# Hybrid trunk step: one weight stream over five expert buffers, the overflow chunk as a fixed unit, the last pair's rows added on TensorE, and another key and query stage

## The reference

```python
def token_mixing(h, p, lru_h0, ctx_ckv, ctx_kr):
    z = h @ p['w_in']                       # Fourier, RG-LRU, short convolution, latent attention
    ...
    q = rmsnorm(einsum(rmsnorm(q_c, g_qa), w_qb), g_qn)   # 8 heads of 64 + 32 channels
    ckv = rmsnorm(kv_c, g_kva)
    k, v = mla_kv(ckv, k_r, w_kvb, g_kn)    # rms over 64 per-head + 32 shared rotary channels
    q, k = rope_tail(q), rope_tail(k)       # latent tokens only: the 32 tail channels are rotated
    ...                                     # 128 cached context keys are appended
    out = sum(gates * branches) @ w_out

def hier_moe(h, p):                         # 4 groups of 8 experts, top 1 group, top 2 experts
    a, u = t @ w1[e], t @ w3[e]             # 1024 -> 256, for each of 32 experts
    y = (silu(a) * u * combine) @ w2[e]     # 256 -> 1024
```

## Time and profile before

| | |
|---|---|
| median of three runs | 1210.94 us (1210.21 to 1211.07) |
| profiled execution, its own time | 1212.13 us |
| its span, first to last instruction | 1210.1 us |
| mean granted TensorE clock | 0.929 |
| TensorE matmul busy | 1019.2 us (84%) |
| VectorE, ScalarE, GpSimd busy | 352.9, 207.0, 190.5 us |
| DMA | 201.34 MB, mean 166 GB/s over the span |

### The profile page before, as it was taken

The page is one execution under the profiler, slowest core; times in us unless marked ns, Lnnn a source line. Parts: engine busy times, 40 slices in busy tenths (PEclk is TensorE's granted clock), DMA queues, the critical chain, the costliest instruction groups (busy, mean ns, idle before and its releaser), DMA issues.

```text
span 1210.1 us, 10632 instructions
## 1 busy us (share of the span) xinstructions
PE 1019.2 (84%) x4116; PEld 582.2 (48%) x4116; DVE 352.9 (29%) x689; ACT 207.0 (17%) x376; POOL 190.5 (16%) x185
## 2 busy tenths in 40 slices
PE   3899989977699899999999999899456987887770
PEld 1455545634355467777777777445432332332320
DVE  4214331235445413233223332134410111111116
ACT  3104430022155410111011111011001111111110
POOL 0000100024520111213131221011010110111102
PEclk9999999989799999999999999899568998899995
DMA  9552551020000252122212121701545899999936
GB/s 374 236 197 93 196 199 44 1 81 0 1 1 1 88 221 84 44 87 69 71 45 95 44 96 60 305 35 60 201 134 209 317 425 425 426 424 427 421 159 260
DMA packets 34657, 201.34 MB, mean 166 GB/s; under 512 B 7408, under 2 KB 11184, under 8 KB 22960
## 3 DMA queue, kind: packets, MB, share of 16 engines
q1 hardware_dynamic: 29840, 190.17, 39.8%
q0 software_dynamic: 4768, 10.49, 2.5%
HBM read 193.37 MB, written 14.09 MB: 171 GB/s over the span
## 4 chain that ended last, share of the span: by engine, by line
PE 80%; DVE 7%; issue 5%; DMA 4%; ACT 2%; POOL 2%; SPq 0%; ACTq 0%; DVEq 0%; POOLq 0%
PE psum L878 20%; PE psum L999 11%; PE psum L623 8%; PE psum L895 7%; PE psum L929 6%; PE psum L1015 5%; PE psum L739 3%; PE psum L815 2%; DMA r_w<-in_w_ada 2%; PE psum L624 2%; PE psum L632 2%; PE psum L829 2%; PE psum L839 2%; PE psum L726 1%; PE psum L773 1%
## 5 line engine op out<-in xcount | busy, mean ns | idle before, releaser
L878 PE MATMUL psum<-r_h,r_w 128*128 128x320 f32 x512 | 143.3, 433 | 1.7 <-DVE r_d L1594 1.7
L1927 POOL TENSOR_TENSOR r_w<-r_w 128x512 f32<-128x512 f32 x64 | 80.6, 1270 | 315.5 <-PE psum L878 240.4
L878 PEld LDWEIGHTS psum<-r_h,r_w 128*128 128x128 f32 x512 | 97.2, 190 | 42.4 <-DVE r_d L1594 2.0
L878 PE MATMUL psum<-r_ys,r_w 128*128 128x320 f32 x384 | 108.6, 432 | 0.0
L623 PE MATMUL psum<-r_h,r_w 128*128 128x512 f32 x192 | 100.2, 604 | 1.5 <-DVE r_h L1376 1.5
L878 PEld LDWEIGHTS psum<-r_ys,r_w 128*128 128x128 f32 x384 | 73.0, 190 | 30.4
L999 PE MATMUL psum<-r_a,r_ckv 128*64 128x512 f32 x128 | 68.2, 694 | 19.8 <-issue 18.6
L1237 ACT ACTIVATE r_bv<-r_bv 128x320 f32<-128x320 f32 x64 | 30.1, 470 | 272.8 <-DVE r_bv L1641 272.8
L929 PE MATMUL psum<-r_w,r_bv 128*128 128x512 f32 x160 | 72.1, 612 | 3.4 <-DVE r_bv L1636 3.4
L999 PE MATMUL psum<-r_w,lruw 128*64 128x512 f32 x128 | 59.1, 616 | 17.0 <-issue 17.0
L999 PE MATMUL psum<-r_c,r_ckv 128*64 128x512 f32 x128 | 68.3, 695 | 0.0
(11 more groups left out here) (342 smaller groups left out, 1499.6 us busy)
## 6 DMA issues: line engine op xcount, KB each, us to landing
r_a<-in_w_ada SPq DMA_DIRECT2D x8, 2048.0 KB, 8.0
r_w<-in_w_gate SPq DMA_DIRECT2D x32, 512.0 KB, 4.5
r_a<-in_w_e SPq DMA_DIRECT2D x8, 2048.0 KB, 17.7
r_c<-in_w_e SPq DMA_DIRECT2D x8, 2048.0 KB, 23.1
r_w<-in_w_e SPq DMA_DIRECT2D x8, 2048.0 KB, 20.4
r_ys<-in_w_e SPq DMA_DIRECT2D x8, 2048.0 KB, 24.8
r_a<-in_w_e SPq DMA_DIRECT2D x8, 1024.0 KB, 20.1
r_c<-in_w_e SPq DMA_DIRECT2D x8, 1024.0 KB, 23.1
```

Of the source, the lines that this page charges most:

```text
L878: ins = mm(gate_bank(u, n), w[:, k, :], x[:, k, :], start=(k == 0), stop=(k == HK - 1))
L1927: g.tensor_tensor(w_mix[n], x, y, op).then_inc(s_wm, 1)
```

## The change

**Key and query stage.** The power of -0.5 on GpSimd becomes a square root on ScalarE (`head_root`; scale and epsilon are folded into it, so L1541 and L1559 go) and a reciprocal on VectorE. The shared rotary squares are summed by ScalarE with the latents. The query tails are rotated before the rms scale, from tables `q_rope` that hold cosine and sine times the gain: three products and one sum on GpSimd instead of seven instructions. The key-value weights get a place of their own in `r_s` (`wkv`) and are loaded early, so `vk0` waits for `ct0` alone; `ct4` comes after `vk0`, and `rt` after `kt3`. In the query stage `take_queries(t - 1)` stands ahead of the reciprocal.

**Experts.** The chunk becomes unit 8 of 17 (`EXTRA`), with one expert read from a register; further chunks (there are none here) would run before the last unit. `STREAM` lists all 33 expert weights in order and uses five buffers in turn, the fifth being `r_bv`. The chunk's own gather, weights and scatter go. `y_d` is cleared by ten stores of zeros early on, behind the modulation rows' store.

**End.** The last unit's rows are not scattered. SP reads `y_d` back once the unit before it is stored; TensorE adds the two rows of each token by products with the identity (`add_rows`) and the last pair's rows by products with a one-hot matrix (`add_last`); VectorE multiplies the sum by the gate row out of PSUM, and VectorE or GpSimd (tiles 0 and 2) adds the residual.

```diff
-RING_USES = [[..., "dft", "wq"], [..., "qkvA", "wkv"],
+RING_USES = [[..., "dft", "wq"], [..., "qkvA"],
-BY_POOL = (0, 1, 2)
+BY_POOL = (0, 2)
+EXTRA = PAIRS // 2
+UNITS_E = [(2 * p, 2 * p + 1) for p in range(PAIRS)]
+UNITS_E.insert(EXTRA, (None,))
+LAST = len(UNITS_E) - 1
+STREAM = [(u, e) for u, es in enumerate(UNITS_E) for e in es]
+AT = [[i for i, (w, _) in enumerate(STREAM) if w == u] for u in range(LAST + 1)]
+TAB_COL = [u if u < EXTRA else PAIRS if u == EXTRA else u - 1 for u in range(LAST + 1)]
+NBUF = 5
...
+        wkv = view(r_s, 0, 2, D)
-        wexp = [r_a[:, 0:EW], r_c[:, 0:EW], r_w[:, 0:EW], r_ys[:, 0:EW]]
+        wexp = [r_a[:, 0:EW], r_c[:, 0:EW], r_w[:, 0:EW], r_ys[:, 0:EW], r_bv[:, 0:EW]]
...
@@ sync
-            ring("wkv", a["w_kv"])
             ring("wq", a["w_q"])
+            sp.wait_ge(s_yl, 2)
+            load("wkv", wkv, a["w_kv"].rearrange("p (k n) -> p k n", k=2))
...
+            sp.wait_ge(s_zero, 1)
+            for i in range(2 * TT):
+                sp.dma_start(y_d[i * P:(i + 1) * P, :], zeros).then_inc(s_clear, 16)
...
             load_w13(3)
             load_w2(3)
+            sp.wait_ge(s_h2d[0], 16 * H2_EARLY)
+            sp.wait_ge(s_lg, 1)
+            load_w13(4)
+            load_w2(4)
...
+            e_x = sp.value_load(xinfo[0:1, 0:1], min_val=0, max_val=NE - 1)
+            for u in range(LAST):
+                after = [i + NBUF for i in AT[u] if i + NBUF < len(STREAM)]
+                if not after:
+                    continue
+                sp.wait_ge(s_A, u + 1)
+                for i in after:
+                    load_w13(i)
+                sp.wait_ge(s_Y, u + 1)
+                for i in after:
+                    load_w2(i)
-            for p in range(PAIRS - 2):
...
             for b in range(2):
-                sp.wait_ge(y_stored[b], 16 * (PAIRS // 2))
+                sp.wait_ge(y_stored[b], 16 * (LAST // 2))
@@ tensor
+            def add_rows(t):
+                pe.wait_ge(yab_loaded[t], 32)
+                o = psum[:, Y_SLOT[t], :]
+                for i in range(2):
+                    for n in range(2):
+                        mm(o[:, n * 512:(n + 1) * 512], ident, yab[t][:, i, n * 512:(n + 1) * 512],
+                           start=(i == 0), stop=False)
+            def add_last(t):
+                o = psum[:, Y_SLOT[t], :]
+                for n in range(2):
+                    ins = mm(o[:, n * 512:(n + 1) * 512], last_hot[:, t * P:(t + 1) * P],
+                             y_sb[:, LAST % 2, n * 512:(n + 1) * 512], start=False, stop=True)
+                ins.then_inc(s_cmb, 1)
...
+                if u < LAST:
+                    pair_T(u + 1)
+                else:
+                    add_rows(0)
+                pe.wait_ge(s_hid, u + 1)
+                hidden_T(gate_e[:, u % 2, :]).then_inc(s_hf, 1)
...
+            add_rows(1)
+            pe.wait_ge(s_ya, LAST + 1)
+            pe.wait_ge(s_yd, LAST + 1)
+            add_last(0)
+            add_last(1)
+            for t in range(2, TT):
+                add_rows(t)
+                add_last(t)
@@ scalar
+            def head_root(n):
+                act.wait_ge(s_krs, n + 1)
+                A(rs[:, n % 2, :], rs[:, n % 2, :], ACT.Sqrt, scale=1.0 / QK,
+                  bias=tiny("sskr", n, 1) if n < KT else tiny("eps")).then_inc(s_hr, 1)
+            for t in range(KT):
+                keys_act(t)
+                head_root(t)
+                if t:
+                    keys_T(t - 1)
@@ vector
-                v.tensor_scalar(rs[:, b, :], rs[:, b, :], 1.0 / QK, EPS, ALU.mult, ALU.add).then_inc(s_krs, 1)
+                if t:
+                    take_queries(t - 1)
                 dve.wait_ge(s_hr, n + 1)
+                step(v.reciprocal(rs[:, b, :], rs[:, b, :]))
+                dve.wait_ge(s_qrope, t + 1)
...
-                step(v.tensor_tensor(yab[t][:, 1, :], yab[t][:, 1, :], yab[t][:, 0, :], ALU.add))
-                ins = v.tensor_tensor(yab[t][:, 1, :], yab[t][:, 1, :], g2_row[:, k, :], ALU.mult)
+                v.tensor_tensor(yab[t][:, 0, :], psum[:, [0, 3, 1, 2, 0][t], :], g2_row[:, k, :], ALU.mult) \
+                    .then_inc(s_ysum, 1)
@@ gpsimd
+                g.tensor_tensor(turn[:, 0], tail, spread(q_rope[:, 0, t, :], 1, H), ALU.mult)
+                for x, y in swapped:
+                    ins = g.tensor_tensor(turn[:, 1, :, x], tail[:, :, y], spread(q_rope[:, 1, t, x], 1, H), ALU.mult)
+                step(ins)
+                g.tensor_tensor(tail, turn[:, 0], turn[:, 1], ALU.add).then_inc(s_qrope, 1)
```

More of the change, by code:

```diff
@@ L1571, in _ @@
                 keys_dve(t)
-            queries_dve(0)
-            for t in range(1, TT):
+            for t in range(TT):
                 queries_dve(t)
-                take_queries(t - 1)
             take_queries(TT - 1)
@@ L1853, in _ @@
             rstd(tiny("ss1"), TT, s_rstd1)
+            pool.wait_ge(loaded["rows"], 16)
+            pool.wait_ge(loaded["consts"], 16)
+            cos, sin = (const(n).rearrange("p (t n) -> p t n", n=HALF) for n in ("cos", "sin"))
+            first, second = slice(0, HALF), slice(HALF, ROPE)
+            gain1, gain2 = (spread(row("gq")[:, x], 1, LT) for x in (first, second))
+            g.tensor_tensor(q_rope[:, 0, :, first], cos, gain1, ALU.mult)
+            g.tensor_tensor(q_rope[:, 0, :, second], cos, gain2, ALU.mult)
+            g.tensor_tensor(q_rope[:, 1, :, second], sin, gain1, ALU.mult)
+            step(g.tensor_tensor(q_rope[:, 1, :, first], sin, gain2, ALU.mult))
+            step(g.tensor_scalar(q_rope[:, 1, :, first], q_rope[:, 1, :, first], -1.0, None, ALU.mult))
             for j in range(2):
@@ L1858, in _ @@
                 g.tensor_tensor(ys[:, j, :], ys[:, j, :], b_sb[:, j, :], ALU.mult).then_inc(s_ys, 1)
-            for t in range(TT):
+            for t in range(LT):
                 pool.wait_ge(s_ssq, t + 1)
@@ new lines, in _, with chunk @@
+            put_rows(LAST - 1)
+            pool.wait_ge(s_slot, 1)
+            n_x = pool.value_load(xinfo[0:1, XCH:XCH + 1], min_val=1, max_val=XCH)
+            pool.sem_inc(x_pause, 1)
+            def chunk(x):
+                pool.wait_ge(x_idx, x * 16)
+                pool.wait_ge(x_pause, 2 * x - 1)
+                pause(2).then_inc(x_pause, 1)
+                gather(x_rows[0:C, :], xtab[0:C, 0:1], x_in)
+                pool.wait_ge(x_yd, x)
+                pool.wait_ge(x_pause, 2 * x)
+                pause(2).then_inc(x_pause, 1)
+                scatter(x_rows[0:C, :], xtab[0:C, 1:2], x_st)
+                pool.wait_ge(x_st, x * 16)
+                pool.wait_ge(x_go, x)
+                pause(3).then_inc(x_go, 1)
@@ L1986, in _tiles @@
+            overflow(pool, n_x, chunk)
+            for t in BY_POOL:
+                pool.wait_ge(s_ysum, t + 1)
+                g.tensor_tensor(x1[:, t, :], x1[:, t, :], yab[t][:, 0, :], ALU.add).then_inc(s_fo[t], 1)
 def _tiles(w, n):
```

377 lines of the change are left out of this document (193 added, 184 removed), and 2 rows, old and new, of the table FRONT.

## The result

The changed kernel takes 1166.73 us in the median of 4 runs (1165.17 to 1167.38), the kernel before 1211.01 us in the same session (1210.21 to 1211.91). The ratio is 0.9632, 95% interval 0.9616 to 0.9649: 3.7% faster. The forecast was 1166. The profiled execution took 1166.28 us, its span is 1164.4, its mean granted clock 0.95 (before: 0.929).

What follows compares the result with a forecast made beforehand. Bounds: a key-and-query-stage ping-pong, expert weight loads with a pause, and a 48.3 us tail. Gains 25.2 + 21.4 - 0.8 = 45.8 us took the median from 1210.94 to 1165, stated as 1166; range 1154 to 1182.

Steps and rivals of the forecast that it cites:

- The start of the key stage: Key and query stage: first key-value product `vk0` starts at 246.5 us instead of 253.05, standing right behind `ct3`.
- TensorE's own work there: Key and query stage: 4.35 us per key tile, 4.8 per query tile, 50 us in all, plus 1 us of waiting.
- Root, reciprocal and their handing over: Key-stage tile chain: ScalarE root with hand-over 0.3 us plus VectorE reciprocal 0.25, together 0.55, bounds 0.3 and 2.0.
- Rival (a): Key stage: hand-overs bound it, each of 11 tiles loses a microsecond, 11 us back, 1177 us; chance 0.13.
- Rival (c): Key stage: ScalarE's roots need table loads, 22 x 1.28 is 28 us, 1194 us; chance 0.03.
- After the last query product: End of key and query stage: square through last `take_queries` takes 7.5 us, so scores start at 305 against 330.21.
- No pause in the stream: Experts: weight loads run without a gap, the 926 to 946 us pause goes, a free buffer some 24 us ahead.
- The stream's length: Experts: 8.31 to 8.5 us per expert, last 2 MB part lands at 1140.4, last `hidden` starts 21.4 us earlier.
- The end: Tail from the start of the last `hidden` to the last store: 49.1 us against 48.3 before, plus 1 us.
- rival (b): Stream at 8.5 throughout (4 us), scatter waits its 10 us (5), TensorE cold in tail (3): 1172 to 1178; chance 0.14.
- (d): Experts: buffers don't help, another wait puts the stream's pause elsewhere, 21 us back, 1187 us; chance 0.05.
- (e): Expert stage: TensorE's clock at 1.2 GHz, units take about 25 us, 130 us added, slower than before; chance 0.03.

## Why the prediction was right, and where it was off

**The start of the key stage.** Right: `vk0` at 246.0, forecast 246.5. The old start cost 8.5 us when it was put back, 1.4 of them through the clock.

**TensorE's own work there.** Right: 4.31 us per key tile against 4.35. From `vk0` to the end of the `qt3` transposes (298.3) it is 52.3 us with 2.2 of waiting, so the 50 us of work hold; the waiting was put at 1.

**Root, reciprocal and their handing over.** 0.30 for the root and 0.20 for the reciprocal, with the hand-overs 0.57 from the sum's end to the reciprocal's (260.66 to 261.23); the term was 0.55. The power put back cost 7.7 us in the stretch, half of what it adds to the chains, as the formula of the forecast has it for a tile without slack. With the 0.4 us of slack that the forecast counted for each key tile the same formula gives 5.6 (0.2 for six key tiles, 0.85 for five query tiles), and TensorE's waits grew by 3.3 us among the keys, 1.6 of them ahead of the very first transposes, a place that the formula does not have. Rival (a) falls: TensorE waited 2.2 us before the last transposes, not 11. Rival (c) falls as well: eleven roots among squares and copies, and no load. The Trainium skill (ScalarE: Activation LUTs, "What ACT_TABLE_LOAD costs") gives 1283 ns for the load itself, and the trace has 1.28; its price for a switch never came due, since there was none.

**After the last query product.** The term was 7.5 us; from the `qt3` transposes at 297.22, which stand right behind that product, to the scores it is 8.4. The sum of the forecast ended its 50 us behind these transposes, though, and from their end it is 7.4. The sum was 305, it was 305.6.

**No pause in the stream.** Right. Four buffers don't make a pause either: what keeps the stream full is that the chunk no longer stands ahead of the loads. The fifth buffer is worth 4.8 us of stream in the profile and 8.7 in the median, with the end's part in it.

**The stream's length.** Here a term was mis-sized. The forecast put the landing of the last 2 MB at 1140.4 in the clock of before, between 1138.0 and 1142.0; it landed at 1117.6 (issued at 1092.42, 25.2 us to landing), which is 1142.5 when 24.9 are added back, just outside. Over the 27.67 experts from the first issue at 881.97 that is 8.52 us each, where the forecast had gone between 8.31 and 8.5. The chain shows where it was lost. From unit 6 to unit 15 there are 17 experts in 142.0 us (959.94 to 1101.93), 8.35 each, as the 8.31 of the middle had it. The last two experts took 15.7 us, 7.9 each. But the 8.67 experts up to unit 6 took 78.0 us, 9.0 each: by the lower sum unit 6 had its weights at 980.1 (919.2 + 7.33 x 8.31), and it was 984.8. So the start of the stream costs more than its middle; the run without rows has it as well (8.0 up to unit 6, 7.4 from there to unit 15). What makes it dearer, no run shows.

To this come 1.5 us between the landing and the product (1.55 in the row shown), which the forecast had called hidden, because TensorE waits for weights there. They are not, for the block for further overflow chunks begins only when unit 15's rows are out of PSUM, and that was as late as the weights. Without the block the two `hidden` stood 1.3 us closer. Together 3.6 us: the last `hidden` gained 17.8 us and not 21.4. Of these, 3.2 were there when unit 15 started (1126.8 in the clock of before, forecast 1123.6); from there on the last `hidden` came by TensorE's own work and the block, and weights that had landed earlier would not have moved it.

**The end.** Mis-sized the other way: 49.1 us were forecast, 45.2 came. The scatter took 4.49 us instead of 5.4; the read-back's first tile was there 5.3 us later, as forecast. The cold start of TensorE, 1.7 us behind the wait in the forecast, fell into the last `hidden` itself (8.6 us instead of 7.1), where the wait for the rows covered it: both together took 9.0 us instead of 10.3, of which the wait, forecast at 3, was 0.43. Behind it nothing was cold. From there to the projection's end it was 8.2 us instead of 9.9, and from then on 28.1 instead of 28.9: the last store ended 3.0 us after the last sum, not 4.0. The old end put back points the same way: 2.7 us slower in the median, 4.0 in the traces, where the forecast had it 0.8 faster.

**The two misses cancel.** Plus 0.3 for the front (24.9 gained, not 25.2), plus 3.6 for the stream and minus 3.9 for the end: the span was met to 0.1 us, its parts were not, and that it was met so closely is luck. In part they are one thing: the late start of the last `hidden` is covered by the chain over the scatter, which fits the small gain of the kernel without the block. Of rival (b) the stream's 8.5 us came true, the slow scatter and the cold projection did not; with four buffers (7.00 and 5.40 us) they nearly did. Rivals (d) and (e) fall with the DMA share of 1.01 and the clock of 0.93 to 0.96 in the stream.

## What to carry to other kernels

A full queue is priced by the bytes that really move; read its rate over the whole way from first issue to last landing, for the start can cost more than the middle (9.0 us an expert against 8.35 here). What stands ahead of a product is hidden behind a wait for weights only if it can begin before the weights land; look at what it waits for itself. Whether a pause disappears depends less on the number of buffers than on what stands ahead of the loads in the issuing queue. And before work is moved off TensorE, look at what it fills: products that bridge a hole of two microseconds can be free, and removing them can cost the clock of what follows.

## What the runs showed of the hardware

**The end of a stream of loads.** The share of the 16 DMA engines is 1.01 until 1100 us, and 0.43 from 1108 to 1117.6, though the last 2 MB issued at 1092.42 have not landed before 1117.6:

```profile
1108.00:1117.60 9.60, 7.68 (x38) 2.94 (x34) 2.02 (x4) 2.10 (x3) 0.00 (x0) 1.00 0.43 182
```

At the full rate the bytes of that stretch would need 4.1 us (9.6 x 0.43). It is 0.44 in the unedited kernel measured again. In the run without row traffic the same 9.6 us ahead of the last landing look otherwise:

```profile
1084.17:1093.77 9.60, 7.26 (x36) 2.83 (x32) 2.02 (x4) 2.10 (x3) 0.00 (x0) 1.00 0.98 415
```

So the fall is not a property of the end as such; it comes with the gathered and scattered rows. The Trainium skill (DMA: Bandwidth & Descriptors, "Why a DMA increments its semaphore by 16 and not by 1") says that a DMA runs on up to 16 engines that finish independently and that the semaphore counts them. The trace agrees. The increments of the last 2 MB's semaphore are spread from 1101.34 to 1117.65, 16.3 us, in the changed kernel, and over 3.0 us (1090.76 to 1093.77) without the rows; for the first 2 MB of the stream they lie 0.8 us apart in both. With the rows the engines drift apart over the stream, and the last one decides when a load has landed. Why the rows weigh unequally on them, no run here shows.

**Contention of VectorE and GpSimd.** Up to 3.02 us instead of 1.23 on the one side, up to 3.33 instead of 2.35 on the other, when both read two operands from SBUF. Not both pay each time: where GpSimd was already at work, its addition kept 2.34 us (1150.38) while VectorE's next to it took 2.40 (1151.39). The Trainium skill (SBUF — State Buffer, "Who interferes with whom") states that a VectorE instruction with two SBUF inputs contends with a GpSimd instruction that reads SBUF, and one with a single SBUF input, outside its two-port modes, does not. The trace agrees: the products with the gate row, one operand from PSUM, kept their 1.21 us beside GpSimd.

**Short waits and the clock.** A wait of 0.43 us ahead of `add_rows(0)` left its products at 3.70 us; with one of 2.38 they took 5.40, at a granted clock of 0.70. Waits of 1.39 and 0.61 us with a small job between them came ahead of a stretch with a granted clock of 0.78; waits of 0.57 and 0.61 us with the products of tile 0 between them left it at 1.00.
